# A four-layer mixer stack with attention and feed-forward: squares added by GpSimd in two norms, and a last norm whose rows are turned early and stored in halves

## What is computed

```python
def rmsnorm(x, g):
    xf = x.astype(jnp.float32)
    y = xf * lax.rsqrt(jnp.mean(xf * xf, axis=-1, keepdims=True) + EPS)
    return (y * g.astype(jnp.float32)).astype(x.dtype)

h = rmsnorm(x, norm_mlp[l])
x = x + jnp.square(jax.nn.relu(h @ w_mlp_in[l])) @ w_mlp_out[l]
return rmsnorm(x, norm_final)
```

## Time and profile before

| | us |
|---|---|
| median of 3 runs | 2649.19 (2649.11 to 2651.65) |
| the profiled execution | 2649.69 |
| its span, first to last instruction | 2648.0 |
| TensorE busy | 2578.6 (97%) |
| VectorE, ScalarE, GpSimd busy | 1521.2, 1231.5, 1513.8 |
| mean granted TensorE clock | 0.992 |

### The profile page before, as it was taken

How to read it: one execution, slowest core, us unless ns; L and a number is a source line. 1 busy time by engine, 2 the same in 40 slices (tenths; PEclk the granted TensorE clock), 3 DMA queues, 4 the chain that set the end, 5 groups by cost and what they waited for, 6 DMA issues and landing times.

```text
span 2648.0 us, 31953 instructions
## 1 busy us (share of the span) xinstructions
PE 2578.6 (97%) x12164; PEld 2081.0 (79%) x12164; DVE 1521.2 (57%) x2431; ACT 1231.5 (47%) x1939; POOL 1513.8 (57%) x926
## 2 busy tenths in 40 slices
PE   8999999999999899999999999989999999999998
PEld 6877787877777687888888787878877778788887
DVE  4999883145675824444450799976498743523202
ACT  4888544245555534222232598654335553423222
POOL 2799765444444365444455299966635547645652
PEclk9999999999999999999999999999999999999999
DMA  5776424444344123333333577533422242233221
GB/s 145 179 179 145 112 96 87 92 95 70 78 78 69 62 80 87 104 96 96 97 96 103 119 180 170 143 96 96 120 96 71 78 136 100 80 99 101 103 96 48
DMA packets 295128, 276.51 MB, mean 104 GB/s; under 512 B 17653, under 2 KB 258511, under 8 KB 294976
## 3 DMA queue, kind: packets, MB, share of 16 engines
q1 hardware_dynamic: 280880, 223.94, 30.9%
q0 software_dynamic: 14096, 50.53, 9.2%
HBM read 228.75 MB, written 5.84 MB: 89 GB/s over the span
## 4 chain that ended last, share of the span: by engine, by line
PE 84%; DVE 9%; ACT 3%; issue 2%; POOL 1%; DMA 0%; DVEq 0%; POOLq 0%; ACTq 0%
PE ps L64 82%; DVE AR L81 4%; PE ps L67 2%; DVE AR L73 2%; DVE HL L81 1%; ACT L70 1%; ACT HT L70 1%; ACT AR L70 1%; DVE X L73 1%; POOL WL L73 0%; POOL AR L73 0%; DMA AR<-in_x 0%; POOL HL L73 0%; DVE AR L77 0%; ACT HH L70 0%
## 5 line engine op out<-in xcount | busy, mean ns | idle before, releaser
L73 POOL TENSOR_TENSOR WL<-WR,WH 128x1024 fp32r<-128x1024 f32 x329 | 831.9, 2549 | 815.0 <-ACT WH L70 815.0
L64 PE MATMUL ps<-HH,WH 128*128 128x512 f32 x3080 | 1228.8, 399 | 22.9 <-POOL HL L73 12.4
L64 PE MATMUL ps<-HL,WH 128*128 128x512 f32 x3080 | 1202.5, 390 | 0.0
L64 PE MATMUL ps<-HH,WL 128*128 128x512 f32 x3080 | 1100.1, 390 | 0.0
L64 PEld LDWEIGHTS ps<-HH,WH 128*128 128x128 f32 x3080 | 580.2, 188 | 167.3 <-issue 33.0
L64 PEld LDWEIGHTS ps<-HL,WH 128*128 128x128 f32 x3080 | 580.7, 189 | 123.6 <-issue 7.7
L64 PEld LDWEIGHTS ps<-HH,WL 128*128 128x128 f32 x3080 | 580.0, 188 | 122.3
L70 ACT ACTIVATE WH<-WR 128x1024 fp32r<-128x1024 f32 (+1 forms) x405 | 409.0, 1047 | 493.0 <-PE ps L64 439.2
L81 DVE SCALAR_TENSOR_TENSOR ps<-AR,CW,ps 128x512 f32<-128x512 f32 x654 | 454.5, 752 | 8.8 <-ACT ps L70 1.5
L73 POOL TENSOR_TENSOR AR<-AR 128x512 f32<-128x512 f32 x200 | 307.9, 1846 | 11.1 <-ACT AR L70 3.8
L70 ACT ACTIVATE AR<-ps 128x512 f32<-128x512 f32 (+3 forms) x265 | 132.2, 523 | 268.2 <-PE ps L64 169.0
(11 more groups left out here) (169 smaller groups left out, 2255.7 us busy)
## 6 DMA issues: line engine op xcount, KB each, us to landing
WR<-in_a_w_in SPq DMA_DIRECT2D x96, 512.0 KB, 5.2
WL<-WR POOLq DMA_DIRECT2D x76, 512.0 KB, 5.8
WR<-in_c_w_in SPq DMA_DIRECT2D x64, 512.0 KB, 5.3
WR<-in_a_w_out SPq DMA_DIRECT2D x16, 1024.0 KB, 4.8
WR<-in_b_w_in SPq DMA_DIRECT2D x16, 1024.0 KB, 8.5
WR<-in_b_w_in SPq DMA_DIRECT2D x32, 512.0 KB, 12.3
WR<-in_w_mlp_in SPq DMA_DIRECT2D x16, 1024.0 KB, 5.4
WR<-in_w_mlp_out SPq DMA_DIRECT2D x16, 1024.0 KB, 4.9
```

The lines of the kernel that those rows point to most:

```text
L64: return Op(None if self.e is None else self.e.matmul(o, l, r, start=first, stop=last, skip_group_check=True))
L73: return Op(None if self.e is None else self.e.tensor_tensor(o, a, b, op))
```

## The change

1. In the norm of A1 (m = 1) and in the last norm (m = 2), rows 0 to 5 of squares are no longer summed by TensorE one by one. ScalarE writes squares of row 0 to RB, of rows 1 to 5 to the two SQ tiles in turn, of rows 6 and 7 to the two DG tiles; GpSimd adds rows 1 to 5 onto RB (`add_squares`, called at the end of its programs for layer C and for the feed-forward part). Squares 3, 4 and 5 wait for the add two rows back.
2. `project_tensor` leaves out the column sums between the banks. Behind the last bank `sum_squares` does three groups: for the added rows, for row 6 and for row 7. For the last norm they go to bank 4 instead of bank 0.
3. In the feed-forward part VectorE scales each row into XG right behind its add, without waiting for the mean square.
4. The transposes use all eight banks (bank 4q + tb). The 16 of q = 0 are issued behind bank 5's matmuls in `project_tensor`; rows 4, 5, 6 of (tb 1, q 1) and (tb 2, q 1) behind bank 7's; the remaining 10 behind the column sums, the last four of them (tb 0, q 1) when bank 4 has been read.
5. Each of the eight banks is one half-row: VectorE and ScalarE evict them in turn in the order DONE, and SyncE stores each with a transfer of 128 rows of 2 KB, eight in all.
6. The norm at the start keeps its way under new names (`first_square`, `first_sum`).

```diff
@@ -469,7 +469,18 @@
 
 
         x0, x_new = sig("x0"), sig("x_new")
-        sq_made, sq_summed = sig("sq_made"), sig("sq_summed")
+        sq_made, sq_acc, sq_summed = sig("sq_made"), sig("sq_acc"), sig("sq_summed")
+
...
         def wait_x(eng, m, k):
             if m == 0:
@@ -477,19 +488,35 @@
             else:
                 eng.wait_ge(x_new, (2, 5)[m - 1], k)
 
+        def squares(k):
+
+            return RB if k == 0 else SQS[k % 2] if k < 6 else DGS[k - 6]
+
         def square(act, m, k):
             wait_x(act, m, k)
-            if k >= 2:
-                act.wait_ge(sq_summed, m, k - 2)
-            act.act(SQS[k % 2], xs(k), ACT.Square).then_inc(sq_made, m, k)
-
-        def sum_square(pe, m, k):
-            pe.wait_ge(sq_made, m, k)
-            column_sums(pe, banks[0][:, 0:NB], SQS[k % 2], k == 0, k == KD - 1).then_inc(sq_summed, m, k)
+            if 3 <= k < 6:
+                act.wait_ge(sq_acc, "x", m, k - 2)
+            act.act(squares(k), xs(k), ACT.Square).then_inc(sq_made, m, k)
+
+        def add_squares(pool, m):
+            for k in range(1, 6):
+                pool.wait_ge(sq_made, m, k)
+                if k > 1:
+                    pool.wait_ge(sq_acc, "x", m, k - 1)
+                pool.tt(RB, RB, squares(k), ALU.add).then_inc(sq_acc, "x", m, k)
+
+        def sum_squares(pe, m):
+            o = banks[0 if m == 1 else 4][:, 0:NB]
+            pe.wait_ge(sq_acc, "x", m, 5)
+            column_sums(pe, o, squares(0), True, False)
+            for k in (6, 7):
+                pe.wait_ge(sq_made, m, k)
+                op = column_sums(pe, o, squares(k), False, k == 7)
+            op.then_inc(sq_summed, m)
 
         def mean_square_vector(dve, m):
-            dve.wait_ge(sq_summed, m, KD - 1)
-            rsqrt_vector(dve, ("ms", m), banks[0][:, 0:NB], NB, 1.0 / D)
+            dve.wait_ge(sq_summed, m)
+            rsqrt_vector(dve, ("ms", m), banks[0 if m < 2 else 4][:, 0:NB], NB, 1.0 / D)
             return small(NB, ("ms", m), 6)
 
 
@@ -539,7 +566,7 @@
         BEFORE = {1: 0, 2: 1, 4: 3, 5: 4}
         BANK_FIRST = {0: 3, 1: 0, 2: 0, 3: 3, 4: 0, 5: 2}
         TILES = {0: KE, 1: KE, 2: KE, 3: KE, 4: KD, 5: 32}
-        sq_row, sq_acc = sig("sq_row"), sig("sq_acc")
+        sq_row = sig("sq_row")
         r_sum, r_v, r_s, r_dve = sig("r_sum"), sig("r_v"), sig("r_s"), sig("r_dve")
         rb_made, rb2_made = sig("rb_made"), sig("rb2_made")
         p_hi, p_lov, p_lop = sig("p_hi"), sig("p_lov"), sig("p_lop")
@@ -622,10 +649,14 @@
                 add(nk - 2, n)
                 wait_tile(nk - 1)
                 add(nk - 1, n).then_inc(p_out, p, n)
-                if p in (2, 5) and n:
-                    sum_square(pe, p // 2, n - 1)
+                if p == 5 and n == 5:
+                    for tb in range(NB):
+                        turn_out(pe, tb, 0, range(4))
+            if p == 5:
+                for tb in (1, 2):
+                    turn_out(pe, tb, 1, (4, 5, 6))
             if p in (2, 5):
-                sum_square(pe, p // 2, 7)
+                sum_squares(pe, p // 2)
 
         def part_scalar(act, p, k, src, wait_h_free):
             s = k % 8
...
@@ -1744,6 +1775,7 @@
             for c in range(2 * KE):
                 split_lo(pool, FIRST_C + c + 1)
             parts_gpsimd(pool, 2, FIRST_A[1] - 8, CY, lambda e, k: e.wait_ge(c_v, k, 7))
+            add_squares(pool, 1)
 
 
         s_row, s_tokv, s_gate, s_fix = sig("s_row"), sig("s_tokv"), sig("s_gate"), sig("s_fix")
@@ -2632,6 +2664,8 @@
                 part_low(dve, 5, k, FH[k])
             for n in range(KD):
                 add_x(dve, 5, n)
+                dve.wait_ge(x_new, 5, n)
+                dve.ts(XG[n], xs(n), va["norm_final"][:, n:n + 1], None, ALU.mult).then_inc(e_xg, n)
 
         def feed_forward_scalar(act):
             for n in range(32):
@@ -2661,43 +2695,48 @@
             for n in range(16):
                 split_lo(pool, FIRST_F + n + 1)
             parts_gpsimd(pool, 5, FIRST_F + 16, FH, lambda e, k: e.wait_ge(f_v, k, 1))
+            add_squares(pool, 2)
 
 
         e_xg, e_t, e_v, e_a, stored = sig("e_xg"), sig("e_t"), sig("e_v"), sig("e_a"), sig("stored")
         XG = [ar(k * T) for k in range(KD)]
         YOUT = [ar(KD * T + tb * D, D) for tb in range(NB)]
 
+        DONE = [(0, 0), (1, 0), (2, 0), (3, 0), (1, 1), (2, 1), (3, 1), (0, 1)]
+
+        def turn_out(pe, tb, q, rows):
+
+            pe.wait_ge(x_new, 5, 4 * q + tb)
+            if (tb, q) == (0, 1):
+                pe.wait_ge(rs_dve, ("ms", 2), "v")
+            for k in rows:
+                pe.wait_ge(e_xg, k)
+                op = pe.turn(banks[4 * q + tb][:, k % 4 * P:(k % 4 + 1) * P], XG[k][:, tb * P:(tb + 1) * P], ident[:, :])
+            if rows[-1] % 4 == 3:
+                op.then_inc(e_t, tb, q)
+
         def finish_tensor(pe):
-            for tb in range(NB):
-                for q in range(2):
-                    if tb >= 2:
-                        pe.wait_ge(e_a if q else e_v, tb - 2)
-                    elif tb or q:
-                        pe.wait_ge(x_new, 5, 2 * tb + q)
-                    else:
-                        pe.wait_ge(rs_dve, ("ms", 2), "v")
-                    for k in range(4):
-                        pe.wait_ge(e_xg, 7)
-                        op = pe.turn(banks[2 * (tb % 2) + q][:, k * P:(k + 1) * P], XG[4 * q + k][:, tb * P:(tb + 1) * P],
-                                     ident[:, :])
-                    op.then_inc(e_t, tb, q)
+            for tb in (1, 2):
+                turn_out(pe, tb, 1, (7,))
+            for tb in (3, 0):
+                turn_out(pe, tb, 1, range(4, 8))
 
         def finish_vector(dve):
             r = mean_square_vector(dve, 2)
-            for k in range(KD):
-                dve.ts(XG[k], xs(k), va["norm_final"][:, k:k + 1], None, ALU.mult).then_inc(e_xg, k)
-            for tb in range(NB):
-                dve.wait_ge(e_t, tb, 0)
-                dve.wait_ge(rs_dve, ("ms", 2), "r")
-                dve.ts(YOUT[tb][:, 0:T], banks[2 * (tb % 2)][:, :], r[:, tb:tb + 1], None, ALU.mult).then_inc(e_v, tb)
+            dve.wait_ge(rs_dve, ("ms", 2), "r")
+            for tb, q in DONE[0::2]:
+                dve.wait_ge(e_t, tb, q)
+                dve.ts(YOUT[tb][:, q * T:(q + 1) * T], banks[4 * q + tb][:, :], r[:, tb:tb + 1], None, ALU.mult).then_inc(
+                    e_v, tb, q)
 
         def finish_scalar(act):
             rsqrt_scalar(act, ("ms", 2), NB)
             r = small(NB, ("ms", 2), 6)
-            for tb in range(NB):
-                act.wait_ge(e_t, tb, 1)
-                act.wait_ge(rs_dve, ("ms", 2), "r")
-                act.act(YOUT[tb][:, T:], banks[2 * (tb % 2) + 1][:, :], ACT.Copy, scale=r[:, tb:tb + 1]).then_inc(e_a, tb)
+            act.wait_ge(rs_dve, ("ms", 2), "r")
+            for tb, q in DONE[1::2]:
+                act.wait_ge(e_t, tb, q)
+                act.act(YOUT[tb][:, q * T:(q + 1) * T], banks[4 * q + tb][:, :], ACT.Copy, scale=r[:, tb:tb + 1]).then_inc(
+                    e_a, tb, q)
 
 
         def sync_program(e):
@@ -2707,11 +2746,11 @@
                 load_chunk(sp, i)
                 if C_GATE + 2 <= i <= C_BR + 1:
                     gates_sync(sp, i - C_GATE - 2)
-            for tb in range(NB):
-                sp.wait_ge(e_v, tb)
-                sp.wait_ge(e_a, tb)
-                sp.dma(out[0, tb * P:(tb + 1) * P, :], YOUT[tb]).then_inc(stored, tb, by=16)
-            sp.wait_ge(stored, NB - 1)
+            for n, (tb, q) in enumerate(DONE):
+                sp.wait_ge(e_a if n % 2 else e_v, tb, q)
+                sp.dma(out[0, tb * P:(tb + 1) * P, q * T:(q + 1) * T], YOUT[tb][:, q * T:(q + 1) * T]).then_inc(
+                    stored, tb, q, by=16)
+            sp.wait_ge(stored, *DONE[-1])
 
         def tensor_program(e):
             pe = Engine(e)
```

More of the change, by code:

```diff
@@ L471, in build_program, with first_square, first_sum @@
         x0, x_new = sig("x0"), sig("x_new")
-        sq_made, sq_summed = sig("sq_made"), sig("sq_summed")
+        sq_made, sq_acc, sq_summed = sig("sq_made"), sig("sq_acc"), sig("sq_summed")
+        def first_square(act, k):
+            act.wait_ge(x0, k)
+            if k >= 2:
+                act.wait_ge(sq_summed, 0, k - 2)
+            act.act(SQS[k % 2], xs(k), ACT.Square).then_inc(sq_made, 0, k)
+        def first_sum(pe, k):
+            pe.wait_ge(sq_made, 0, k)
+            column_sums(pe, banks[0][:, 0:NB], SQS[k % 2], k == 0, k == KD - 1).then_inc(
+                sq_summed, *((0, k) if k < KD - 1 else (0,)))
         def wait_x(eng, m, k):
@@ L736, in setup_tensor @@
                 if k:
-                    sum_square(pe, 0, k - 1)
-            sum_square(pe, 0, KD - 1)
+                    first_sum(pe, k - 1)
+            first_sum(pe, KD - 1)
             pe.wait_ge(small_in, "all")
@@ L778, in setup_scalar @@
             for k in range(KD):
-                square(act, 0, k)
+                first_square(act, k)
```

## The result

The changed kernel took 2640.24 us (median of 5 runs, 2637.17 to 2642.52), the kernel before 2651.24 (5 runs, 2649.11 to 2652.79). The ratio is 0.9955, 95% interval 0.9944 to 0.9966: 12 us faster, with 9 to 15 inside the interval. The two medians are 11.0 us apart. The forecast was 2636.2 with a range of 2634.0 to 2640.5, a gain of 13.0. The profiled execution took 2640.33 us, its span was 2638.6.

The account below looks back on a forecast made before the run. TensorE, busy 97% of a 2648.0 us span, bounds the kernel, so time comes only from its waits or needless work. Last stage 9.0 plus A1's norm 4.0 give 13.0 us: 2649.2 - 13.0 = 2636.2 us, range 2634.0 to 2640.5.

Parts of the forecast that it names:

- The last stage: Last norm and output: column sums leave the banks, rows are scaled and turned early; end at 2639.0 against 2648.0, 9.0 us.
- The output's rate: Output transfers: 2.10 MB at 406 GB/s take 5.2 us, plus 0.1 us for rows of 2 KB; issues 0.35 us apart.
- The collision with the scaled rows: Last stage: VectorE's scaled rows wait for at most one GpSimd add each, row 5 1.0 us late; costed at nothing.
- the scaling of 2100.62: Trace of the kernel before: a VectorE scaling took 5.43 us while GpSimd did four adds; cited as agreeing with the skill's rule.
- A1: Norm of layer A1: banks every 1.36 us, five GpSimd adds at 1.27 us; mean square 4.0 us earlier.
- (a): Rival, both norms: GpSimd adds take 1.74 us each; A1 gains 1.8, the end 8.5, time 2638.9 us; chance 0.16.
- (b): Rival, column sums in both norms: TensorE's clock falls before they are through, up to 2.8 us once, 2639.0 us; chance 0.12.
- a clock of 0.50 inside the sums: Sign of being wrong: TensorE's clock row shows 0.50, that is 1.2 GHz, inside the column sums.
- The sum: Whole kernel: 13.0 us gained in all, 2649.2 - 13.0 = 2636.2 us.
- (c): Rival, output: small transfers don't overlap, eight take 16 us; 9.3 us worse, 2645.5 us; chance 0.06.
- (d): Rival, last stage: each scaled row holds VectorE for a whole GpSimd burst, row 6 17.2 us late, 2653.4 us; chance 0.03.

Follow-up runs that it names:

- the burst: The changed kernel with four additional GpSimd adds on spare tiles ahead of GpSimd's first add of the last stage; span 2643.1 us, last stage 30.32 us.

## Why the prediction was right, point by point

*The last stage.* 9.0 us were forecast and 9.1 measured (9.12, 9.15, 9.17 in three profiles). TensorE's stream between the banks held: 1.36 us a bank, sixteen transposes at 1.79 (I had 1.8), mean square 14.53 us behind the first add where the forecast's times give 14.74. The first transfer was issued at 16.76 us (I had 17.0). GpSimd's adds ended 9.9 us behind the first add, 1.8 us before TensorE asked for them.

*The output's rate.* The term was mis-sized: I took 406 GB/s and 0.1 us for short rows. Rows of 2 KB moved at 375 to 387 GB/s, 0.3 us more for all, as the run with four transfers confirms; the earlier start made up for it, which is luck. The issues came 0.56 us apart and not 0.35 (4.49 us for eight), with the engines full, and a transfer landed 2.0 to 3.1 us after its issue, not over 4.

*The collision with the scaled rows.* Costed at nothing, and it was nothing: add 5 was 0.4 us late, not 1.0, and the sixteen transposes covered it. But the reason that I gave was not needed. I wrote that only one add can be ready at a time; the burst shows that VectorE gets in between adds that are all ready. The rule of the Trainium skill (SBUF — State Buffer, "Who interferes with whom"), that the second of the two blocks for the whole of the first, agrees with the scaled rows of 0.80 to 0.93 us: the row of 2618.03 ended at 2618.96, after a GpSimd add that began at 2617.38. It does not cover the row for which I said that the trace agrees: the scaling of 2100.62 began 0.71 us before GpSimd's first add and stood through four. A hold over four or five operations is more than that rule says, and both came behind a transfer issued by GpSimd.

*A1.* Forecast 4.0 us, measured 3.1 and 3.5. The step that failed is the price of an add: I divided 5.06 by 4, from adds that don't depend on one another, and used it for a chain in which each waits for the last. 5 x 0.14 = 0.7 us. The dearer adds of rival (a), 1.74 us, did not come either, but its direction was right. The other 0.4 in the first profile are sums at the lower clock, my rival (b), which I had priced at 2.8 and given 0.12. I had named a clock of 0.50 inside the sums as a sign of being wrong, and it is there in A1: of the eight profiles with the pause, six lost 0.25 to 1.9 us by it. It belongs into the forecast as a cost that most executions pay in part, not as a case of its own.

*The sum.* 13.0 were forecast; the stages give 12.2 to 12.7, the ratio 12. The median of before that I subtracted from was one of three runs and 2.05 us under that of the five. That, and 2.0 us less between the medians than forecast, make the time 4.0 us longer than my number. It lies inside the range by 0.26 us only, where executions of this kernel went from 2637.17 to 2642.52: that it fell inside is partly luck. It is also nearer to the times of (a) and (b), 2638.9 and 2639.0, than to mine; the time alone would not have told which of the three came true, the lengths of the stages do. The rivals on transfers that don't overlap (c) and on VectorE held at each row (d) are refuted: the engines' share was 1.00 with eight transfers, and no scaled row of the changed kernel's last stage exceeded 0.93 us.

## What to carry to other kernels

Small work that sits in a full TensorE stream costs its whole time; sum it elsewhere and sum it late, but price a chain of dependent operations by a chain. Where an engine waits for one of several inputs of a sum, take the others first: reordering three groups made that norm 1.6 to 2.0 us shorter on top of the 3.1 to 3.5 of the change. When whole times spread by more than the effect, compare the lengths of stages between two events of the trace, but measure again at a later event: of those 1.6 to 2.0 us only 0.7 to 1.3 were left 1150 us further on.

## What the runs showed that I had not expected

A GpSimd add that waits for its predecessor took 1.40 us on average, an independent one 1.26 with no scaled row beside it and 1.47 with scaled rows. VectorE is let in between GpSimd operations that are all ready (scaled rows 0.79 to 0.92 us), but stood 6.64 us behind a transfer issued by GpSimd and the adds after it; why, no run here tells. A transfer of 128 KB costs SyncE 0.48 us, which bounded the output at 265 GB/s. Unchanged stretches ahead of the change differed by 3 us between executions, with the granted clock 0.88 or 0.94, and 0.96 or 1.00, in them. And the same 16 small matmuls, after the same wait of 2.1 us, took from 1.93 to 3.55 us.
